# Group attention of a hybrid decoder layer: moving the copy and sum of the value products, and using three PSUM banks in turn in fewer rounds

## What is computed

```python
xn = rms_norm(h, attn_norm_w[l])
z = xn @ w_in[l]                       # ... | zq | zk | zv | ...
q = rms_norm(zq.reshape(B, S, N_GROUPS, HEADS_PER_GROUP, HEAD_DIM), q_norm_w[l][:, None, :])
k = rms_norm(zk.reshape(B, S, N_GROUPS, HEADS_PER_GROUP, HEAD_DIM), k_norm_w[l][:, None, :])
v = zv.reshape(B, S, N_GROUPS, HEADS_PER_GROUP, HEAD_DIM)
for g, (win, dil) in enumerate(ATTN_GROUPS):      # (128,1), (512,4), (2048,16)
    cols = rel_bias_table[:, g * HEADS_PER_GROUP:(g + 1) * HEADS_PER_GROUP]
    o_g, lse_g = dilated_window_attention(q[:, :, g], k[:, :, g], v[:, :, g], cols, win, dil)
# inside, per block of queries: scores = q k^T * Dh**-0.5 + bias, masked;
# m = max(scores); p = exp(scores - m); l = sum(p); o = (p v) / l
```

## Time and profile before

| | us |
|---|---|
| Median of three runs (1917.82 to 1919.31) | 1917.92 |
| The profiled execution's own time | 1919.12 |
| Its span, first to last instruction | 1917.0 |
| PE busy in the span | 1868.9 (97%) |
| DVE busy | 1201.1 (63%) |
| ACT busy | 758.6 (40%) |
| Mean granted clock of TensorE | 0.996 |

### The profile page before, as it was taken

The page is one execution under the profiler, slowest core; times in us unless marked ns, Lnnn a source line. Parts: engine busy times, 40 slices in busy tenths (PEclk is TensorE's granted clock), DMA queues, the critical chain, the costliest instruction groups (busy, mean ns, idle before and its releaser), DMA issues.

```text
span 1917.0 us, 23710 instructions
## 1 busy us (share of the span) xinstructions
PE 1868.9 (97%) x8789; PEld 1600.1 (83%) x8789; DVE 1201.1 (63%) x1643; ACT 758.6 (40%) x1414; POOL 89.3 (5%) x150
## 2 busy tenths in 40 slices
PE   6999999999999999999999999999999999999999
PEld 5787899889998889888888787877888888888887
DVE  5634653565355488898424625458778787876675
ACT  5423432353134136312712413265545454544443
POOL 1101110111010011000100000000000000000000
PEclk9999999999999999999999999999999999999999
DMA  7421422132222211021012504222232323257543
GB/s 251 143 89 59 134 83 88 66 132 94 86 74 91 87 44 45 1 66 61 24 49 56 189 22 137 94 77 67 66 98 66 98 67 97 66 189 275 168 143 99
DMA packets 133972, 184.15 MB, mean 96 GB/s; under 512 B 15929, under 2 KB 63033, under 8 KB 133881
## 3 DMA queue, kind: packets, MB, share of 16 engines
q1 hardware_dynamic: 125817, 172.33, 27.6%
q10 hardware_dynamic: 8064, 10.59, 1.5%
HBM read 142.92 MB, written 39.96 MB: 95 GB/s over the span
## 4 chain that ended last, share of the span: by engine, by line
PE 86%; DVE 7%; ACT 3%; DMA 1%; issue 1%; SPq 0%; POOL 0%; ACTq 0%; DVEq 0%; POOLq 0%
PE psum L240 28%; PE psum L242 27%; PE psum L241 27%; DVE wlo L198 1%; PE psum L511 1%; PE psum L814 1%; DMA grp<-group_out 1%; DVE softstat L1185 1%; PE psum L367 1%; PE psum L1028 1%; ACT sc L1091 1%; DVE pt_lo L1199 0%; DVE grp L1525 0%; DVE sc L1183 0%; ACT q_hi L521 0%
## 5 line engine op out<-in xcount | busy, mean ns | idle before, releaser
L240 PE MATMUL psum<-whi,act_lo 128*128 128x512 f32 x768 | 316.9, 413 | 15.6 <-DVE q_lo L525 13.3
L241 PE MATMUL psum<-wlo,act_hi 128*128 128x512 f32 x768 | 305.6, 398 | 0.0
L242 PE MATMUL psum<-whi,act_hi 128*128 128x512 f32 x768 | 305.4, 398 | 0.0
L240 PEld LDWEIGHTS psum<-whi,act_lo 128*128 128x128 f32 x768 | 194.7, 254 | 32.8 <-DVE q_lo L525 14.8
L242 PEld LDWEIGHTS psum<-whi,act_hi 128*128 128x128 f32 x768 | 195.0, 254 | 16.1
L241 PEld LDWEIGHTS psum<-wlo,act_hi 128*128 128x128 f32 x768 | 195.9, 255 | 13.5
L240 PE MATMUL psum<-act_hi,wlo 128*128 128x512 f32 x512 | 202.2, 395 | 0.0
L242 PE MATMUL psum<-act_hi,whi 128*128 128x512 f32 x512 | 199.6, 390 | 0.0
L241 PE MATMUL psum<-act_lo,whi 128*128 128x512 f32 x512 | 199.3, 389 | 0.0
L193 ACT CAST whi<-stage 128x512 fp32r<-128x512 f32 x200 | 120.5, 622 | 175.5 <-PE psum L242 166.3
L198 DVE TENSOR_TENSOR wlo<-stage,whi 128x512 fp32r<-128x512 f32 x200 | 129.4, 688 | 94.1 <-ACT whi L193 93.3
(11 more groups left out here) (252 smaller groups left out, 3513.4 us busy)
## 6 DMA issues: line engine op xcount, KB each, us to landing
stage<-in_w_in SPq DMA_DIRECT2D x144, 256.0 KB, 4.0
u_raw<-in_w_up SPq DMA_DIRECT2D x44, 512.0 KB, 5.1
stage<-in_w_down SPq DMA_DIRECT2D x44, 256.0 KB, 4.0
w_sums<-stage SPq DMA_DIRECT2D x44, 256.0 KB, 2.5
gated_scratch<-g_buf SPq DMA_DIRECT2D x22, 512.0 KB, 2.6
gated<-gated_scratch SPq DMA_DIRECT2D x44, 256.0 KB, 3.7
d_raw<-w_sums SPq DMA_DIRECT2D x44, 256.0 KB, 2.7
d_raw<-in_w_down SPq DMA_DIRECT2D x33, 256.0 KB, 3.5
```

What stands on the lines that cost most here:

```text
L240: nc.tensor.matmul(dst, lhs[1], rhs[0], start=first, stop=False, skip_group_check=True)
L241: nc.tensor.matmul(dst, lhs[0], rhs[1], start=False, stop=False, skip_group_check=True)
L242: return nc.tensor.matmul(dst, lhs[0], rhs[0], start=False, stop=last, skip_group_check=True)
```

## The change

Three edits go together. First, banks in turn only in rounds that can have value products: `in_turn_of_three` now begins at the fifth Q tile (rounds 20 and 44) instead of the first, and the formula of the bank runs the other way round; the first GEMM after the rounds in turn (28 and 52) writes bank 3, which the scores have left, with a wait for `s_read`. The wait for `hn_lo` is now made in rounds 21 to 27 and 45 to 51, and not in 18 to 20, 28, 42 to 44 and 52. Second, ACT makes the copy of the value products of tile i-4 ahead of the exponentials of tile i-2. Third, DVE makes the sum ahead of the low half of the probabilities of tile i-3. No instruction of PE, ACT or DVE is added or taken away.

```diff
-            return 0 <= g < NG - 1 and pos >= 2 * NT or 0 < g < NG and pos < 4
+            return 0 <= g < NG - 1 and pos >= 2 * NT + 4 or 0 < g < NG and pos < 4
+
+        def third_bank(i):
+            return 2 * (i - 2 * NT - 4) % 3
 ...
-            return (i + 2) % 3 if in_turn_of_three(i) else index % 2
+            if in_turn_of_three(i):
+                return third_bank(i)
+            return 3 if i in (3 * NT + 4, 6 * NT + 4) else index % 2
 ...
-            return (i + 4) % 3 if in_turn_of_three(i + 1) else 2
+            return third_bank(i + 2) if in_turn_of_three(i + 1) else 2
 ...
-                self.low_bank = 6 if kind == "Q" and g == NG - 1 else gemm_bank(self.index)
+                self.low_bank = 6 if kind == "Q" and g == NG - 1 else third_bank(i + 3)
 ...
-                    if in_turn_of_three(i - 1) and i - 2 in part and tiles[i - 2].kind != "V":
+                    if in_turn_of_three(i) and in_turn_of_three(i - 1):
                         pe.wait_ge(hn_lo, tiles[i - 2].n + 1)
-
-                    if tl.kind == "K" and tl.g and tl.t == 5:
+                    if tl.kind == "K" and tl.g and tl.t == 4:
+                        pe.wait_ge(s_read, NT * tl.g)
+                    if tl.kind == "K" and tl.g and tl.t == 6:
                         pe.wait_ge(o_read, 2 * NT * tl.g)
 ...
-                    if earlier and earlier.paired and earlier.low_bank < 3:
+                    if earlier and earlier.paired and in_turn_of_three(i):
                         pe.wait_ge(o_read, 2 * earlier.a + 2)
 ...
@@ tiles_act: moved from behind the store of tile i - 5 to ahead of the exponentials of i - 2
+                tl = tile_of(part, i - 4, "Q")
+                if tl:
+                    act.wait_ge(o_done, tl.a + 1)
+                    if tl.a >= 2:
+                        act.wait_ge(o_stored[tl.a % 2], per_tile * (tl.a // 2))
+                    for b, (main, _) in enumerate(pair_parts(tl)):
+                        copied = nc.scalar.copy(pair_dst(tl)[:, 2 * b:2 * b + 2, :], main)
+                    copied.then_inc(o_read, 1)
 ...
@@ tiles_dve: moved from behind the low half of the probabilities of i - 3 to ahead of it
+                tl = tile_of(part, i - 4, "Q")
+                if tl:
+                    dve.wait_ge(o_read, 2 * tl.a + 1)
+                    for b, (_, cross) in enumerate(pair_parts(tl)):
+                        dst = pair_dst(tl)[:, 2 * b:2 * b + 2, :]
+                        total = nc.vector.tensor_tensor(dst, cross, dst, ALU.add)
+                    total.then_inc(o_read, 1)
```

More of the change, by code:

```diff
@@ L1116, in tiles_act @@
                         "p a h -> p (a h)")).then_inc(o_stored[tl.t % 2], 16)
[L1117 to L1124, removed]
                 tl = tile_of(part, i - 4, "X")
@@ L1200, in tiles_dve @@
                                             ALU.subtract).then_inc(pt_lo_done, 1)
[L1201 to L1207, removed]
                 free_time()
```

## The result

| | before | after |
|---|---|---|
| median of the runs, us (lowest to highest) | 1917.87 (1917.61 to 1919.31), 4 runs | 1902.09 (1901.19 to 1902.90), 4 runs |
| profiled execution, us | 1919.1 | 1901.4 |
| span, us | 1917.0 | 1899.2 |
| PE busy, us | 1868.9 | 1864.4 |

The ratio is 0.9916 with a 95% interval of 0.9904 to 0.9928: 15.8 us less, where 14.8 was forecast. The changed kernel was timed once more beside the later experiments, as `a_changed`: 1901.06 us (1899.25 to 1904.29) against 1917.82, ratio 0.9916 [0.9902, 0.9929].

A forecast was written before the change was run, and what follows sets the result against it. PE, busy 97% of the span, bounds the kernel, so its 19.3 us of attention-stage waits were the target: 8.9 - 1.0 + 4.8 + 0.0 + 1.4 + 0.7 = 14.8 us off 1917.9 gave 1903.1, range 1899.7 to 1908.5.

The forecast's parts named there:

- Part 1: Rounds 18 to 20 and 42 to 44: q_lo waits go with the new banks, 8.9 us, less 1.0 us cost.
- DVE's lateness: GEMM 21 and 45: DVE's queue delivers q_lo late, 0.36 and 0.6 us, cost 1.0 us, bounds 0 and 2.4.
- Part 2: Attention rounds: copy and sum moved, all seven ob waits go, 4.8 us; the copy has 0.6 us margin before the exponentials.
- Part 3: Weight rounds 23 and 47: GEMM 24 waits about 1.45 us, GEMM 48 3.1; net 0.0 us, bounds +1.8 and -1.5.
- this as a bound: Weight round 23: weights in group 0 as slow as in group 1, GEMM 24 waiting some 1 us longer; within -1.5 us.
- Part 4: Behind GEMM 24 and 48: TensorE's clock stays high in group 0, gaining 1.4 us, and low in group 1.
- the first rival: Low clock stays in group 0, or comes once elsewhere, with no wait covering it: 1904.5 to 1906 us; chance 0.2.
- Part 5: End of group 2, round 71: qn wait of 0.4 goes, pt_lo wait shrinks by 0.3; 0.7 us, bounds 0 and 1.2.
- The second: Attention rounds: chain closes at pt_lo and DVE's queue delays GEMMs, so 4.8 and 1.4 go: about 1909 us; chance 0.11.
- The third: Behind GEMM 24 and 48: both low-clock stretches go, another 1.6 us, 1901.5 us; chance 0.08.
- The fourth: PE stands still as long at other waits, such as GEMM 19's bank: within 3 us of 1917.9; chance 0.04.
- The fifth: Late copy delays exponentials over 2.7 us, pt_lo misses value products: 1923 us at one us beyond; chance 0.02.

The follow-up runs named there:

- e2: The changed kernel with ACT's copy and DVE's sum back in their old places, so the bank edit alone: 1908.51 us, ratio 0.9956.
- e4: The changed kernel with ACT's copy back at the end of its round, so of the two moves only DVE's sum is early: 1910.05 us, ratio 0.9963.
- e3: The changed kernel with DVE's sum back behind pt_lo, so of the two moves only ACT's copy is early: 1908.40 us, ratio 0.9951.
- e1: The kernel before with the moves of copy and sum alone, banks as before: 1911.43 us, ratio 0.9965.
- e5: The changed kernel with ACT's copy into ob made six times in a row: 1919.47 us, ratio 1.0004.
- e9: The kernel of e8 with DVE's last four weight cuts also behind the add and maximum of the scores: 1892.89 us, ratio 0.9866.
- e7: The changed kernel with DVE's subtractions that stood ahead of q_lo moved to before pt_lo: 1898.43 us, ratio 0.9899.
- e10: The changed kernel with ACT's copy into ob made three times in a row: 1902.55 us, ratio 0.9916.
- e6: The changed kernel with four of the eight weight cuts moved behind q_hi on ACT and q_lo on DVE: 1896.12 us, ratio 0.9885.
- e8: The changed kernel with the edits of e6 and e7 together: 1893.60 us, ratio 0.9871.

## Why the prediction was right, and where it was not

The time fell inside the range, and the mechanism is the forecast one, but for the clock and the landing of the weights. That the sum came so near is partly luck: the clock gave 1.2 us less than forecast and the other parts 3.2 more. The terms, each against the table of rounds:

| part | forecast | measured |
|---|---|---|
| 1: q_lo waits, less DVE's lateness | 8.9 - 1.0 = 7.9 | 10.26 - 1.18 = 9.1 |
| 2 and 3: ob waits and both weight rounds | 4.8 + 0.0 | 4.69 + 0.37 - 0.10 + 1.65 = 6.6 |
| 4: low clock in group 0 | 1.4 | 0.17 |
| 5: end of group 2 | 0.7 | 0.93 |
| sum | 14.8 | 16.8 |

**Part 1: right, and mis-sized by the reading of idle time.** The six waits and nothing else went (e2 alone shows it). Each gave more than its row: the row of 1.63 gave 1.87, 1.62 gave 1.77 and 1.81, 1.19 gave 1.47. The idle time is counted from the modelled end of the matmul before, 0.60 us behind the start of the transposes, while a GEMM that need not wait starts 0.36 us behind it (161.14 and 161.50 above). So a wait that follows pipelined matmuls costs 0.24 us more than its brackets say. The single waits gave 0.15 to 0.28 more than their brackets: the six of Part 1 together 1.38, the five ob waits outside the weight rounds 1.08 (4.69 against 3.61). That is most of the 3.2 us. DVE's lateness was forecast as 0.36 and 0.6 us of waits; they are 0.36 and 0.55, and as lengths of rounds 0.46 and 0.72. One reading was loose without harm: I wrote "about 6 us" for qn, and 215.59 plus 0.68 less 209.63 is 6.64, which left 0.9 us of margin and not 1.5.

**Part 2: right, margin and all.** The copy ended 0.63 us ahead of the first exponential where 0.6 was forecast, no ob wait is left, and the transposes of rounds 21 and 22 are 10.06 us apart (191.42, 201.48) instead of 11.03. I had put PE's own work at 10.31 from the 0.72 in the row; the same 0.25 us is missing there. e4 shows what I had not said: the sum's gain hangs on the copy's move.

**Part 3: the net was near, the two halves were not.** For GEMM 24 I forecast 1.45 and it was 2.39 (2.11 in the repeat), over the 2 us that I had named as a sign of being wrong: relative to the issue of their loads the cuts start 0.84 us earlier, and the seventh load landed 10.41 us behind the first issue (215.33 against 204.92) instead of 9.45 (222.27 against 212.82), with the store of ob issued among the loads in both. I had named this as a bound and not taken it: the time that the change took out ahead of the cuts was the cover of these transfers. For GEMM 48 I forecast 3.1 and it was 2.17 (2.78 in the repeat, where the round lasted 12.91 instead of 12.32). The subtractions ahead of it end 10.63 us behind the transposes of round 45 (381.74 plus 1.41 against 372.52), as forecast, which is worth the 0.7. What I took for fixed was the way from there to the landed weights, which leads through SP's queue. SP's issues in before, and below them those of after with the rows of the 10.63:

```profile
398.17 3.65 SPq L1241 DMA_DIRECT2D w_sums<-stage  x4
401.92 0.90 SPq L186 DMA_DIRECT2D stage<-in_w_in  x2
...
372.52 0.60 PE L516 MATMUL psum<-ident,qn 128*128 128x128 f32 x4
381.74 1.41 DVE L752 TENSOR_TENSOR stage<-stage 128x512 f32<-128x512 f32 x2
383.18 1.80 SPq L1247 DMA_DIRECT2D w_sums<-stage  x4
385.07 2.30 SPq L186 DMA_DIRECT2D stage<-in_w_in  x3
```

The same in six profiled executions (us; the three columns called behind are counted from the end of the subtractions):

| kernel | subtractions end | longest issue of a store | issue of the first load | behind: first load issued | behind: second load issued | behind: eighth load landed | GEMM 48 waits |
|---|---|---|---|---|---|---|---|
| before | 398.14 | 2.33 | 0.40 | 3.8 | 4.2 | 13.24 | 3.10 |
| e2_banks_only | 388.00 | 1.76 | 0.38 | 3.2 | 3.6 | 12.19 | 2.03 |
| e3_act_move | 388.72 | 2.02 | 0.40 | 3.5 | 3.9 | 12.42 | 2.26 |
| e1_moves_only | 393.12 | 0.46 | 1.36 | 1.9 | 3.3 | 12.15 | 2.23 |
| after | 383.15 | 0.47 | 1.32 | 1.9 | 3.3 | 12.11 | 2.17 |
| after, repeat | 381.43 | 0.45 | 1.46 | 1.9 | 3.4 | 12.72 | 2.78 |

In each of them one issue lasts 1.3 to 2.3 us and ends 2.9 to 3.4 us behind the subtractions. In before, e2 and e3 it is a store; in the three with both moves it is the first load, so of the 1.9 us by which that load goes out sooner only 0.9 is left at the second. (In e5, with both moves and six copies, it is again a store, with 1.09 us.) The wait follows the landing of the eighth load: it is 10.1 to 10.2 us less in the first three kernels and 9.9 less in the other three. So the fall from 3.10 to 2.17 is a landing 1.1 us sooner, less 0.2. It can't be put down to the moves: e2 has neither and waited 2.03, and the two executions of after differ by 0.6. What held SP, and why the loads of before landed latest, was not tried. GEMM 24 goes by the same landing in the kernels with both moves: 12.98, 12.71 and 12.51 us behind the subtractions of round 21 in after, its repeat and e1, with waits of 2.39, 2.11 and 1.93, 10.6 less each time.

**Part 4: wrong, the first rival came true.** The clock fell again behind both waits; the windows behind GEMM 24 and 48 of after, beside the earlier trace rows (PEclk is the number ahead of the last two):

```profile
218.00:222.00 4.00, 3.39 (x8) 2.76 (x9) 3.96 (x6) 1.13 (x6) 1.01 (x1) 0.57 0.64 229
398.00:403.00 5.00, 5.00 (x15) 4.32 (x16) 3.61 (x6) 2.55 (x9) 0.29 (x1) 0.66 0.53 190
```

The step that failed was the chance: I counted seven waits of nine behind which the clock had stayed, as if they were alike. The seven were not the two of the earlier trace rows, and these two had remained in the kernel. The half of the step that said the loss was covered was right. In e3, where the clock in group 0 did stay high, the ob wait of round 24 came out of its cover and the round lasted 11.92 us as before:

```profile
221.75 0.63 PE L240 MATMUL psum<-whi,act_lo 128*128 128x512 f32 x1 [1.30 <-DVE q_lo L530]
229.07 0.66 PE L516 MATMUL psum<-ident,qn 128*128 128x128 f32 x4 [1.29 <-DVE ob L1212]
...
220.00:227.00 7.00, 5.70 (x26) 5.55 (x26) 4.64 (x6) 3.54 (x11) 1.57 (x2) 1.00 0.70 249
```

In after nothing covers it, and it costs 11.80 - 10.35 = 1.45 us in round 24 and 10.62 - 9.15 = 1.47 in round 48 (against e9). That the waits are the cause is shown as far as this: the low clock came behind both waits in before, after, its repeat, e1, e2, e4, e5, e7 and e10, behind GEMM 48 alone in e3, and never in this stage in e6, e8 and e9, which lack these waits. The stretches of e8, in the place of the two above:

```profile
215.00:221.00 6.00, 6.00 (x30) 6.00 (x29) 5.74 (x9) 2.73 (x10) 0.43 (x1) 1.00 0.82 271
391.00:398.00 7.00, 7.00 (x35) 6.93 (x35) 5.61 (x10) 3.97 (x14) 0.25 (x1) 1.00 0.74 243
```

Why 1.30 us kept the clock in e3 while 1.31 in before and in e2 did not, no run here tells. The rule of the Trainium skill that I had weighed (TensorE: Matmul & The Clock Gate, section on a second failure mode) would have let both stretches go with the many short waits. The trace does not agree: fourteen of the waits went, only two of 0.36 and 0.55 us came, and both stretches stayed.

**Part 5: right** to 0.2 us, but not as forecast: the qn wait of 0.38 is gone and the pt_lo wait only shrank from 0.84 to 0.77, not by 0.3. The other 0.5 of the 0.93 stands in no bracket; 0.28 of it is that the value products start 0.38 us behind their transposes instead of 0.66, for which the rows give no reason.

**The rivals.** The first came true in its mechanism, but the 3.2 us that the sum had left out elsewhere hid it, so the time fell below the forecast and not above. The second, that DVE's queue takes the gain, is what remains in small: 1.2 us at GEMM 21 and 45. The third needed the waits at GEMM 24 and 48 gone, as e8 shows. The fourth was excluded by e1 and e2. The fifth is real, as e5 shows, but my place and point for it were wrong: I let it decide from 3.3 us at the value products, and it decides from 2.2 us at the transposes of the probabilities ahead of them.

## What to carry to other kernels

When a wait goes, read which queue its chain ran through and what else stands in that queue ahead of the needed instruction: here the order within DVE and ACT (cuts ahead of q_lo, subtractions ahead of it) held a further 9.6 us of the stage, and moving work into an idle time ahead of another wait cost nothing. A move on one engine that only pays with its counterpart on another must be tried as one edit; the half of it can cost what it was to save (e4 against e2: no gain by the medians, 2.4 us longer in the stage). And before a transfer is taken as hidden, subtract from its cover what the change takes out of the kernel ahead of it.

## What the runs showed of the hardware

- The low clock cost 1.45 and 1.47 us once nothing covered it, and in this stage it came only behind waits of 1.3 to 3.7 us: those at GEMM 24 and 48, and in e4 once more behind the pt_lo wait of 2.04 us near the end. Length alone doesn't decide: the waits of 1.63 us in rounds 18 and 42 (before and e1) and one of 2.11 us for pt_lo in e5 (at 254 us, granted clock 1.00 in the 6 us behind it) did not bring it.
- Removing a wait behind pipelined matmuls gave 0.15 to 0.28 us more than the idle time in its row (eleven waits).
- The eight weight loads (256 KB each) that are cut in round 23 of after took 3.6 us to land for the first and 7.2 us for the last, with two stores of the output issued among them. The waits that hang on them scatter: that at GEMM 48 was 2.17 and 2.78 us in two profiled executions of the changed kernel, that at GEMM 24 2.39 and 2.11.
- The wait for weights went by the landing of the last load and not by the issue of the first: at GEMM 48 it was 10.1 to 10.2 us less than that landing in before, e2 and e3, and 9.9 less in e1, after and its repeat.
